# Expert weights laid out with a partition's rows side by side in HBM, and products that step through their moving operand to match

## The reference, cut to what matters

```python
h = jax.nn.silu(jnp.einsum('td,edf->tef', x, wg)) * jnp.einsum('td,edf->tef', x, wu)
h = h * combine[..., None].astype(h.dtype)
return jnp.einsum('tef,efd->td', h, wd)
```

## Time and profile before

| | us |
|---|---|
| Median of 3 runs | 1393.22 (1388.38 to 1394.91) |
| The profiled execution's own time | 1394.18 |
| Its span in the trace | 1392.5 |
| TensorE busy | 1170.4 (84%) |
| VectorE busy | 410.0 (29%) |
| ScalarE busy | 264.8 (19%) |
| GpSimd busy | 233.5 (17%) |
| Share of SP's queue of 16 DMA engines' time | 65.2% |

### The profile page before, as it was taken

The page is one execution under the profiler, slowest core; times in us unless marked ns, Lnnn a source line. Parts: engine busy times, 40 slices in busy tenths (PEclk is TensorE's granted clock), DMA queues, the critical chain, the costliest instruction groups (busy, mean ns, idle before and its releaser), DMA issues.

```text
span 1392.5 us, 27311 instructions
## 1 busy us (share of the span) xinstructions
PE 1170.4 (84%) x10800; PEld 779.9 (56%) x10801; DVE 410.0 (29%) x1141; ACT 264.8 (19%) x544; POOL 233.5 (17%) x405
## 2 busy tenths in 40 slices
PE   6998788999989789987769799989988799999630
PEld 4676555576757645553437576767656455555310
DVE  0025646412431632221112203331423422222115
ACT  0005631202320411110001213022202211111011
POOL 2004992000000012222112100000000022222122
PEclk9999989999999889998879899999998799999875
DMA  9646789843587559999999303443697198999941
GB/s 331 235 143 212 234 263 364 296 147 115 189 293 278 213 197 374 349 399 397 397 394 369 122 0 142 164 168 134 231 379 266 55 398 324 397 398 398 397 151 37
DMA packets 159954, 360.34 MB, mean 259 GB/s; under 512 B 9623, under 2 KB 11687, under 8 KB 159882
## 3 DMA queue, kind: packets, MB, share of 16 engines
q1 hardware_dynamic: 146994, 331.50, 65.2%
q0 software_dynamic: 12752, 27.69, 5.7%
q10 hardware_dynamic: 144, 0.27, 0.1%
HBM read 341.47 MB, written 18.38 MB: 258 GB/s over the span
## 4 chain that ended last, share of the span: by engine, by line
PE 68%; DVE 9%; DMA 8%; SPq 6%; issue 4%; ACT 4%; POOL 0%; POOLq 0%; DVEq 0%; ACTq 0%
PE acc L708 37%; PE psS L708 13%; PE psV L708 6%; SPq L664 5%; PE psN L708 5%; DMA ring<-in_w_exp_down 3%; DVE feats L1407 2%; PE acc L1002 2%; DMA feats<-in_w_exp_down 1%; PE psN L1109 1%; PE acc L811 1%; DMA arena<-by_slot,arena 1%; ACT feats L2023 1%; DMA ring<-in_w_in_even 1%; ACT arena L1283 1%
## 5 line engine op out<-in xcount | busy, mean ns | idle before, releaser
L708 PE MATMUL acc<-feats,ring 128*128 128x288 f32 x1280 | 317.4, 411 | 11.2 <-ACT feats L1943 4.2
L708 PEld LDWEIGHTS acc<-feats,ring 128*128 128x128 f32 x1280 | 245.8, 193 | 81.4 <-issue 10.1
L2146 POOL DMA_DIRECT2D by_slot<-feats x208 | 103.3, 497 | 556.4 <-DVE feats L1784 318.5
L708 PE MATMUL psS<-ring,feats 128*32 128x256 f32 x2176 | 140.2, 415 | 46.9 <-issue 46.9
L708 PEld LDWEIGHTS psS<-ring,feats 128*32 128x32 f32 x2176 | 74.9, 120 | 101.9 <-issue 66.4
L708 PE MATMUL psS<-arena,feats 128*32 128x256 f32 x1408 | 89.8, 404 | 26.2 <-issue 25.7
L1776 DVE TENSOR_TENSOR feats<-feats,psS 64x256 f32<-64x256 f32 x52 | 22.1, 425 | 265.2 <-ACT feats L2033 265.2
L708 PE MATMUL psN<-arena,feats 128*32 128x256 f32 (+1 forms) x1360 | 83.4, 379 | 13.0 <-DVE feats L1742 13.0
L1283 ACT ACTIVATE arena<-acc 128x1024 f32<-128x1024 f32 (+7 forms) x98 | 72.3, 757 | 112.2 <-PE acc L708 34.7
L2033 ACT ACTIVATE feats<-psS 64x256 f32<-64x256 f32 x52 | 19.5, 375 | 353.9 <-PE psS L708 353.9
L708 PEld LDWEIGHTS psS<-arena,feats 128*32 128x32 f32 x1408 | 46.0, 116 | 59.9 <-issue 36.2
(11 more groups left out here) (336 smaller groups left out, 1284.7 us busy)
## 6 DMA issues: line engine op xcount, KB each, us to landing
ring<-in_w_exp_gate SPq DMA_DIRECT2D x22, 2048.0 KB, 16.9
ring<-in_w_exp_up SPq DMA_DIRECT2D x22, 2048.0 KB, 21.7
ring<-in_w_exp_down SPq DMA_DIRECT2D x22, 2048.0 KB, 19.6
arena<-in_w_exp_gate SPq DMA_DIRECT2D x10, 2048.0 KB, 18.3
arena<-in_w_exp_up SPq DMA_DIRECT2D x10, 2048.0 KB, 22.6
feats<-in_w_exp_down SPq DMA_DIRECT2D x10, 2048.0 KB, 19.9
ring<-in_cache_k SPq DMA_DIRECT2D x64, 256.0 KB, 3.2
ring<-in_cache_v SPq DMA_DIRECT2D x64, 256.0 KB, 3.2
```

The lines of the kernel that those rows point to most:

```text
L708: return pe.matmul(out, lhsT, rhs, start=first, stop=last)
L2146: pool.dma_start(by_slot[rows, 256 * q:256 * q + 256], YS[32 * q:32 * q + 32, at]).then_inc(S.stored, 16)
```

## The change: a layout of the expert weights and the steps that match it

The DRAM side of the three weight loads is split as `(p k) n` instead of `(k p) n`. Partition p then holds rows 8p to 8p + 7 of a gate or up matrix and rows 4p to 4p + 3 of a down matrix: 16 KB that lie side by side in HBM. The place in SBUF of slice k stays the same.

The contraction over features must pair the same features on both sides. So slice k of the chunk's rows is now the columns 8m + k of `XTOK`, m = 0 to 127: `pick` reads its moving operand in steps of 8 columns (32 bytes), two runs of 128 for each column tile. For the down product, slice s of the hidden columns must be the columns 4m + s: `gate_and_up` reads its moving operand in steps of 4 columns (16 bytes), again two runs of 128. Counts of instructions, the sizes, the waits and `down` itself are unchanged.

```diff
--- before.py
+++ after.py
@@ -662,7 +662,7 @@
                     where, landed, _ = place(l, p, j)
                     w = (w_exp_gate, w_exp_up, w_exp_down)[j]
                     sp.dma_start(where.rearrange("p (k n) -> p k n", k=(8, 8, 4)[j]),
-                                 w[l, bass.ds(e, 1)].rearrange("a (k p) n -> p (a k) n", p=P)).then_inc(landed, 16)
+                                 w[l, bass.ds(e, 1)].rearrange("a (p k) n -> p (a k) n", p=P)).then_inc(landed, 16)
 
                 def expert(e, p):
 
@@ -1099,7 +1099,8 @@
                 pe.wait_ge(S.table, c + 1)
                 for t in range(3):
                     for q in range(4):
-                        last = mm(psN[32 * q:32 * q + 32, 0:256], PT[:, t, :], XTOK[:, t, 256 * q:256 * q + 256], t == 0, t == 2)
+                        last = mm(psN[32 * q:32 * q + 32, 0:256], PT[:, t, :],
+                                  XTOK[:, t, :].rearrange("p (m k) -> p k m", k=8)[:, 2 * q:2 * q + 2, :], t == 0, t == 2)
                 last.then_inc(S.picked, 1)
 
             def turn_picked(S, c):
@@ -1116,7 +1117,8 @@
                 for k in range(8):
                     for q in range(4):
                         last = mm(psS[32 * q:32 * q + 32, 0, 0:256], XS[:, k % 2, 32 * (k // 2):32 * (k // 2) + 32],
-                                  (Wg, Wu)[q // 2][:, k, 256 * (q % 2):256 * (q % 2) + 256], k == 0, k == 7)
+                                  (Wg, Wu)[q // 2][:, k, :].rearrange("p (m s) -> p s m", s=4)[:, 2 * (q % 2):2 * (q % 2) + 2, :],
+                                  k == 0, k == 7)
                 last.then_inc(S.gate_up, 1)
 
             def turn_h(S, c):
```

## The result

| | before | after |
|---|---|---|
| Median, us | 1393.6 (1388.38 to 1394.91, 4 runs) | 1603.12 (1600.29 to 1606.95, 4 runs) |
| Span of the profiled execution, us | 1392.5 | 1604.5 |

The ratio is 1.151, 95% interval 1.147 to 1.155. The kernel became 15% slower; the forecast was 1375 us. The first rival came true, in the form that doubles the price of a read.

What follows compares the result with a forecast made beforehand. Weight loads were taken to bound the ends of both expert stages. Gains of 11 and 6.5 us, 17.5 together, gave 1376.7 from 1394.18; 0.96 for the median and 0.7 for the clock gave 1375 us, range 1366 to 1435.

Steps and rivals of the forecast that it cites:

- The first rival: Strided gate, up and pick reads cost TensorE time as four tiles stream at once; doubled, about 1580 us; chance 0.25.
- the price of the strided read: Gate, up and pick, 5.0 us per chunk: bounded between nothing and a doubling, taken as zero from VectorE's rows.
- 187 us: Loss if strided reads double: 52 chunks by 5.0 us, less 40.7 + 31.9 us that gate and up stand idle.
- the rate forecast: Full weight-load queue with 16 KB packets: 423 GB/s, bounds 388 and 429, from a straight line through shorter packets.
- Rival 2: Weight loads no faster, as joined runs are cut again or HBM sets 388 to 407 GB/s; 1390 us; chance 0.13.
- Layer 0's 11 us: Layer 0's expert stage: ten back-to-back expert loads, each 1.1 us shorter, give 11 us.
- Layer 1's 6.5 us: Layer 1's expert stage: the queue runs dry before expert 12's load, so the last load lands only 6.5 us earlier.
- third rival: Chunk stores on POOL's queue starve behind 16 KB packets, deciding from 0.7 us on; 1434 us; chance 0.09.
- the first rival's rule: Extra time per chunk acts on 28 chunks before the last queues form: 8 in layer 0, 20 in layer 1.

Runs made afterwards that it cites:

- e2: The changed kernel with its strided reads kept but the weight loads as before (2 and 4 KB packets); 1619.70 us, ratio 1.164.
- e6: The kernel before, with the q, k, g and a projections (one moving stream) reading in steps of 8 columns; 1466.28 us, one run.
- e1_loads_only: The changed kernel with its 16 KB loads kept but TensorE's reads unstepped as before; 1399.34 us, ratio 1.006.
- e3: The changed kernel with pick, gate and up reading columns in pairs, which ScalarE's copy and VectorE's product put apart; 1383.58 us, ratio 0.9945.
- e20: e3 with 4 of the 8 steps of gate and up products left out in layer 1 alone; 1381.32 us, ratio 0.9913.
- e7_runs_8kb: The changed kernel with all weights in two 8 KB runs, gate and up read unstepped, pick in pairs; 1378.57 us, ratio 0.9914.
- e8: The changed kernel with all weight runs 4 KB, TensorE's reads as before and ScalarE's copy as in e3; 1381.92 us, ratio 0.9934.
- e13: e7_runs_8kb with down fetched in 16 KB runs as in e3, and gate and up read in pairs; 1385.58 us, ratio 0.9946.

## Why the prediction was wrong

**The step that failed** is the price of the strided read: "It takes about 1 ns per element; one of TensorE's four concurrent streams takes 3.64 us / 16 / 256 = 0.9 ns per column. At nearly the same pace I take the value zero." The argument went from VectorE to TensorE by their pace per element. VectorE indeed reads float32 in steps of 32 bytes for nothing; TensorE at about that pace needs twice the time (e2, e6). A like pace was no evidence of a like way of reading. The rule of the Trainium skill that the prediction names said otherwise, and I set it aside by rows of another engine.

**The first rival** had the right size and the wrong cause. A doubling was its upper end, and 7.53 and 3.00 us are just over it. By its own sum, 187 us become 208 when each chunk grows by 5.41 us and not by 5.0: 52 x 0.41 = 21 us. Four streams at once were its cause, but a single one pays (e6). It should have had the largest chance, since the only row against it came from another engine; as it was, 0.16 of it lay beyond the range.

**The runs do come about, at the rate forecast.** Of the 90321 packets of the changed kernel 12359 have 8 KB or more, and 96 matrices by 128 are 12288. With the read mended they go at 428 to 433 GB/s, where I estimated 423. Rival 2 is out.

**Layer 0's 11 us**: from the load that waits for expert 0 to the gather, e1_loads_only, whose layer 0 has the same chunks, takes 234.3 us, 10.0 less than the kernel before; e3 takes 236.3, 8.0 less. So that term held to within 1 us, with stores that land in 6.2 us in e1 as well. e1 reads without a step; e3's pairs cost TensorE 0.27 us in each of the 8 chunks ahead of the queue, 2.2 us, about what lies between the two.

**Layer 1's 6.5 us**: 2.3 in e3. The term rested on chunks as long as before. With stores of 10.2 us, the third rival's mechanism, they are longer, and behind them stands TensorE, close enough that shorter stores alone don't help. TensorE's own chunk is longer too: by the first rival's rule, 28 chunks by 0.27 us of the pairs are 7.6 us, about as much as e3 lacks. No run takes the pairs' price alone out of layer 1, so how the missing 8 us divide between the pairs and the stores is not shown. e20 shows only that with TensorE far shorter the stores still hold layer 1 where it was. The rival was to decide from 0.7 us on and does not: a chunk's stores take 2.6 us more in e3, and it is still faster than before. My reading, argued from the two chains and not tested by itself, is that the delay counts only within experts of several chunks, and that the quicker loads make up for it between them.

## A version that beats both

e7_runs_8kb computes what the reference asks and took 1378.57 us, 0.9% under the kernel before. The intervals of e3, e8 and e13 overlap its own, so which of the four is best is open; each interval lies below 1, and each kernel some 220 us under the changed one. The simplest is e8: it needs no stepped read on TensorE at all, and its stores land as before.

## What to carry to other kernels

When a layout is changed so that a DMA gets longer runs, look at how TensorE will read it: keep at least two neighbouring float32 columns together, and let an engine that reads PSUM anyway put them in order. A price for one engine is not evidence for another; the nearest row must be of the same engine, or the bound stays open. And before a faster load is booked in full, ask how long the next two chains per step are: here they were some 2 us apart, and each hid what cutting the other was worth.

## What the runs showed that I had not expected

- TensorE's moving operand in float32: 16 and 32 bytes apart one by one, twice the time; 8 bytes apart, or in pairs 16 and 32 bytes apart, some 5% more (64 products in 3.80 to 3.86 us against 3.64 to 3.66, 24 in 1.54 to 1.59 against 1.47 to 1.48). VectorE shows none of it, though from SBUF only on copies of 32 elements.
- A store on another queue waits among the long packets of a full one: 4.7 us with packets of 2 and 4 KB, 5.1 with 8, 6.3 with 16, and a hardware queue (ScalarE's, 6.9 us) does it no better than POOL's.
- One core's loads hold 428 to 433 GB/s for tens of us with 16 KB packets. The Trainium skill (DMA: Bandwidth & Descriptors, Where 436 GB/s comes from) has the memory bind a core near 358 GB/s; with one core at work these traces don't agree with that sentence.
